# Turning the Delta layer's inputs to tokens block by block, two blocks behind their convolution

## The reference

```
u, qkv, g_in, beta_in, z = split(a @ w_in)
y_ssm = s5_glu(u, ...)                      # hg * sigmoid(hg @ w_glu + b_glu)
qkv = silu(causal_conv(qkv, conv_w))        # 4 taps along the tokens
q, k, v = split(qkv, 3)
q = l2norm(q per head) * 128 ** -0.5
k = l2norm(k per head)
beta = sigmoid(beta_in)
g = -exp(a_log) * softplus(g_in + dt_bias)  # summed along each chunk
o = gated_delta_chunked(q, k, v, g, beta)
```

## Time and profile before

| what | value |
|---|---|
| median of 3 runs | 3237.29 us (3222.32 to 3237.57) |
| the profiled execution's own time | 3239.65 us |
| its span, first to last instruction | 3238.1 us |
| mean granted TensorE clock | 0.945 |
| TensorE busy (matmul) | 2942.9 us, 91% |
| VectorE busy | 1127.9 us, 35% |
| ScalarE busy | 631.1 us, 19% |

### The profile page before, as it was taken

One profiled execution on the slowest core, in us unless ns is written; L12 is line 12 of the kernel. 1 busy time (PEld: TensorE's weight loads), 2 busy tenths in 40 slices (PEclk: granted clock), 3 DMA queues, 4 the chain that ended last, 5 costly groups with the idle time before them and its releaser, 6 DMA issues. The chain is left out here.

```text
span 3238.1 us, 32792 instructions
## 1 busy us (share of the span) xinstructions
PE 2942.9 (91%) x12473; PEld 1583.8 (49%) x12474; DVE 1127.9 (35%) x2447; ACT 631.1 (19%) x1248; POOL 246.2 (8%) x352
## 2 busy tenths in 40 slices
PE   7999899999799999979799899577897999999798
PEld 5544555545444444434376644367654444444243
DVE  2584355544200000024371623566464000000052
ACT  3310355521100101112211111222211101101030
POOL 0000000001100000020000000134201000000110
PEclk9999899999799999989897799888997999999899
DMA  4000881031699999962110210000414999999641
GB/s 153 26 27 0 328 347 53 1 121 57 241 414 415 421 405 399 397 243 84 52 50 1 37 44 26 1 2 2 165 53 169 415 413 412 410 404 397 235 162 45
DMA packets 138550, 617.24 MB, mean 191 GB/s; under 512 B 25188, under 2 KB 31748, under 8 KB 121992
## 3 DMA queue, kind: packets, MB, share of 16 engines
q1 hardware_dynamic: 110952, 525.93, 41.2%
q0 software_dynamic: 24064, 86.00, 7.0%
q10 hardware_dynamic: 3376, 3.19, 0.3%
HBM read 508.00 MB, written 105.91 MB: 190 GB/s over the span
## 5 line engine op out<-in xcount | busy, mean ns | idle before, releaser
L1974 PE MATMUL acc<-wg,xt 128*128 128x512 f32 x512 | 222.9, 598 | 0.0
L737 PE MATMUL acc<-h,xt 128*128 128x512 f32 x384 | 165.2, 592 | 0.0
L2572 PE MATMUL acc<-xt,slabs 128*128 128x512 f32 x384 | 165.1, 592 | 0.0
L1974 PEld LDWEIGHTS acc<-wg,xt 128*128 128x128 f32 x512 | 98.5, 193 | 123.2 <-issue 123.2
L376 PE MATMUL scores<-qkt 65*128 65x512 f32 (+7 forms) x384 | 148.9, 498 | 0.9 <-DVE qkt L516 0.9
L522 DVE TENSOR_REDUCE nmax<-scores 128x1 f32<-128x256 f32 (+7 forms) x128 | 96.8, 756 | 77.5 <-PE scores L378 76.2
L1720 PE MATMUL py<-place 128*64 128x512 f32 (+1 forms) x352 | 120.2, 594 | 1.0 <-DVE place L1800 1.0
L1720 PE MATMUL pu<-place 128*128 128x512 f32 (+1 forms) x320 | 119.8, 593 | 0.0
L2572 PEld LDWEIGHTS acc<-xt,slabs 128*128 128x128 f32 x384 | 72.9, 190 | 91.4 <-issue 91.4
L737 PEld LDWEIGHTS acc<-h,xt 128*128 128x128 f32 x384 | 72.9, 190 | 91.1 <-issue 90.9
L1243 PE MATMUL acc<-place 128*128 128x512 f32 x256 | 114.3, 601 | 2.7 <-PEq L75 2.7
(11 more groups left out here) (645 smaller groups left out, 5170.1 us busy)
## 6 DMA issues: line engine op xcount, KB each, us to landing
own<-in_moe_w_gate_dram SPq DMA_DIRECT2D x22, 2048.0 KB, 16.3
place<-in_moe_w_down_dram SPq DMA_DIRECT2D x22, 2048.0 KB, 16.3
place<-in_moe_w_up_dram SPq DMA_DIRECT2D x20, 2048.0 KB, 18.2
slots_out<-zeros SPq DMA_DIRECT2D x4, 9216.0 KB, 62.8
place<-in_moe_w_gate_dram SPq DMA_DIRECT2D x18, 2048.0 KB, 21.2
own<-in_moe_w_up_dram SPq DMA_DIRECT2D x16, 2048.0 KB, 16.0
own<-in_moe_w_down_dram SPq DMA_DIRECT2D x10, 2048.0 KB, 19.5
xt<-in_moe_w_gate_dram SPq DMA_DIRECT2D x9, 2048.0 KB, 22.4
```

Source lines behind the costliest of these rows:

```text
L737: last = pe.matmul(acc[:, n % 4, 0:width], xs[:, k, tile_of(i)], weights[:, k, cols], start=(k == 0), stop=(k == k_of - 1))
L1974: last = pe.matmul(acc[:, u % 4, :], xt[:, k, i * P:(i + 1) * P], wg[:, k, n * SLAB:(n + 1) * SLAB], start=(k == 0), stop=(k == KD - 1))
L2572: last = pe.matmul(acc[:, n % 4, :], slabs[:, s % 2, k, (m % 4) * P:(m % 4 + 1) * P], xt[:, k, half * SLAB:(half + 1) * SLAB], start=(k == ...
```

## The change

`gdn_to_tokens` is gone, and with it the second of the stages above. `delta_inputs` takes the place of `project_convolved` and does both jobs by blocks of 128 channels. Between the two products of block m TensorE turns block m - 2 (8 transposes into two PSUM banks, `tokens`); ScalarE copies it to its place in token order with one operation over 1024 columns; VectorE squares and sums it behind the convolution of block m; ScalarE takes its 8 roots one block later, and VectorE scales it. The factor of q is folded into the sum before the root. `gdn_masks`, `load_rows` and `gdn_gates` stand in the same joint stage as `s5_glu` and `delta_inputs`: 29 semaphores and one meeting. The gates' matmul (`sums`) stands on TensorE behind block 0, their copy (`sums_out`) on VectorE ahead of the first convolution. Places move too: q, k and v lie in `h` and `gdn_t`, and a new `work` of 12 blocks holds the weight slabs, the gate's input and later what `h`, `gdn_t` and `qkv` held.

```diff
--- before.py
+++ after.py
-def s5_glu(nc, c, t, j, y, out_t, joint):
+def s5_glu(nc, c, t, j, y, hgt, sig, out_t, joint):
-        hgt = sbuf(nc, ctx, "hgt", [P, KC, S])
-        sig = sbuf(nc, ctx, "sig", [P, 2, SLAB])
...
-def project_convolved(nc, c, xt, w, conv_w, out_t, joint):
+def delta_inputs(nc, c, xt, w, conv_w, slabs, squares, qkv, sums, sums_out, joint):
...
+        out = sbuf(nc, ctx, "out", [P, 3, S])
+        taps_raw = out[0:GDN_CONV].rearrange("p a n -> p (a n)")[:, 0:3 * GDN_W]
+        ms, length = [sbuf(nc, ctx, n, [P, NORMED, NT]) for n in ("ms", "length")]
         acc = psum(nc, ctx, "acc", [P, 4, SLAB])
...
+        tokens = psum(nc, ctx, "tokens", [P, 2 * SLAB])
+        with stage(nc, "slab0_in", "slab1_in", "taps_in", "taps_turned", "taps_out", "products", "copied", "convolved",
+                   "activated", "turned", "to_tokens", "squared", "roots", "vec_steps", joint=joint) as (
+                       block, (slab0_in, slab1_in, taps_in, taps_turned, taps_out, products, copied, convolved, activated, turned,
+                               to_tokens, squared, roots, vs)):
...
+            def place(m):
+                return qkv[m // GDN_HEADS][:, :, m % GDN_HEADS, :]
             @block.sync
             def _(sp):
...
+                sp.dma_start(taps_raw, conv_w).then_inc(taps_in, 16)
...
+                    sp.dma_start(slabs[s % 2], w_v[:, :, s * SLAB:(s + 1) * SLAB]).then_inc(slab_in[s % 2], 16)
             @block.tensor
             def _(pe):
+                def product(m, half):
...
+                def turn(m):
+                    pe.wait_ge(activated, m + 1)
+                    if m:
+                        pe.wait_ge(to_tokens, m)
+                    else:
+                        pe.wait_ge(taps_out, 2)
+                    for i in range(NT):
+                        last = pe.transpose(tokens[:, i * P:(i + 1) * P], out[:, m % 3, i * P:(i + 1) * P], c.ident[:])
+                    last.then_inc(turned, 1)
                 pe.wait_ge(taps_in, 16)
                 for m in range(blocks):
...
+                    last = pe.transpose(tokens[:, m * GDN_CONV:(m + 1) * GDN_CONV], taps_raw[:, m * P:(m + 1) * P], c.ident[0:GDN_CONV, 0:GDN_CONV])
                 last.then_inc(taps_turned, 1)
                 for m in range(blocks):
...
+                        pe.wait_ge(slab_in[m // 4 % 2], 16 * (m // 8 + 1))
+                    product(m, 0)
+                    if m >= 2:
+                        turn(m - 2)
+                    product(m, 1)
+                    if m == 0:
+                        sums(pe, tokens[:, SLAB:SLAB + NT * GDN_HEADS])
+                turn(blocks - 2)
+                turn(blocks - 1)
             @block.scalar
             def _(act):
+                def evacuate(m, half):
+                    act.wait_ge(products, 2 * m + half + 1)
+                    if m >= 2:
+                        act.wait_ge(convolved, m - 1)
+                    act.activation(raw[:, m % 2, PAD + half * SLAB:PAD + (half + 1) * SLAB], acc[:, (2 * m + half) % 4, :], ACT.Copy).then_inc(copied, 1)
                 def silu(m):
                     act.wait_ge(convolved, m + 1)
...
+                    act.activation(out[:, m % 3, :], out[:, m % 3, :], ACT.Silu).then_inc(activated, 1)
+                def copy(m):
+                    act.wait_ge(turned, m + 1)
+                    act.activation(place(m), tokens[:].rearrange("p (t d) -> p t d", t=NT), ACT.Copy).then_inc(to_tokens, 1)
+                def root(m):
+                    act.wait_ge(squared, m + 1)
+                    act.activation(length[:, m, :], ms[:, m, :], ACT.Sqrt).then_inc(roots, 1)
                 for m in range(blocks):
...
+                    evacuate(m, 0)
+                    if m >= 2:
+                        copy(m - 2)
+                    if 3 <= m < NORMED + 3:
+                        root(m - 3)
+                    evacuate(m, 1)
                     if m:
                         silu(m - 1)
                 silu(blocks - 1)
+                copy(blocks - 2)
+                copy(blocks - 1)
             @block.vector
             def _(dve):
                 step = Steps(dve, vs)
...
+                def convolve(m):
                     dve.wait_ge(copied, 2 * m + 2)
-                    o = out_t[m]
+                    if m >= 3:
+                        dve.wait_ge(turned, m - 2)
+                    o = out[:, m % 3, :]
...
+                def lengths(m):
+                    dve.wait_ge(to_tokens, m + 1)
+                    step(dve.tensor_tensor(squares, place(m), place(m), ALU.mult))
+                    step(dve.tensor_reduce(ms[:, m, :], squares, AX.X, ALU.add))
+                    dve.tensor_scalar(ms[:, m, :], ms[:, m, :], EPS, float(GDN_HD) if m < GDN_HEADS else 1.0, ALU.add, ALU.mult).then_inc(squared, 1)
+                def scale(m):
+                    dve.wait_ge(roots, m + 1)
+                    step(dve.reciprocal(length[:, m, :], length[:, m, :]))
+                    step(dve.tensor_tensor(place(m), place(m), length[:, m, :].unsqueeze(2).to_broadcast([P, NT, GDN_HD]), ALU.mult))
+                dve.wait_ge(taps_turned, 1)
+                dve.tensor_copy(taps[:].rearrange("p m a -> p (m a)"), tokens[:, 0:blocks * GDN_CONV]).then_inc(taps_out, 1)
+                dve.wait_ge(taps_out, 1)
+                sums_out(dve, tokens[:, SLAB:SLAB + NT * GDN_HEADS]).then_inc(taps_out, 1)
+                dve.memset(raw[:, 0, 0:PAD], 0.0)
+                step(dve.memset(raw[:, 1, 0:PAD], 0.0))
+                for m in range(blocks):
+                    convolve(m)
+                    if 2 <= m < NORMED + 2:
+                        lengths(m - 2)
+                    if 3 <= m < NORMED + 3:
+                        scale(m - 3)
...
+def gdn_gates(nc, c, t, j, gb, g, joint):
...
+        with stage(nc, "in", "negated", "exped", "logged", "summed", "vec_steps", joint=joint) as (
...
-                dve.wait_ge(summed, 1)
-                step(dve.tensor_copy(g.sums[:], ps[:]))
...
+            def sums(pe, out):
                 pe.wait_ge(logged, 1)
+                pe.matmul(out, c.upto[:], s[:].rearrange("p t h -> p (t h)"), start=True, stop=True).then_inc(summed, 1)
+            def sums_out(dve, out):
+                dve.wait_ge(summed, 1)
+                return dve.tensor_copy(g.sums[:].rearrange("p t h -> p (t h)"), out)
+    return sums, sums_out
...
-def gdn_to_tokens(nc, c, qkvt, qkv, joint):
...
-        qkvt = [h[:, m] for m in range(NT)] + [gdn_t[:, m] for m in range(4)]
-        with joint_stage(nc) as joint:
-            s5_glu(nc, c, t, j, output_of(u), s5_t, joint)
-            project_convolved(nc, c, xt, w_in[:, OD_QKV:OD_G], t["gdn_conv_w"][j], qkvt, joint)
         def tiles(block4):
             return block4.rearrange("p k n -> p (k n)").rearrange("p (t h d) -> p t h d", t=NT, h=GDN_HEADS)
-        wt, qt, scratch = tiles(h[:, 0:4]), tiles(h[:, 4:8]), tiles(gdn_t[:])
+        qkv = (tiles(h[:, 0:4]), tiles(h[:, 4:8]), tiles(gdn_t[:]))
...
+            work = sbuf(nc, heads, "work", [P, 12, S])
+            wt, qt, scratch = [tiles(work[:, n:n + 4]) for n in (0, 4, 8)]
...
             with ExitStack() as prepare:
+                k = Masks()
+                gdn_mask_places(nc, k, prepare)
                 with joint_stage(nc) as joint:
-                    k = gdn_masks(nc, c, prepare, joint)
+                    gdn_masks(nc, c, k, joint)
+                    sig = sbuf(nc, joint.memory, "sig", [P, 2, SLAB])
+                    s5_glu(nc, c, t, j, output_of(u), work[:, 8:12], sig, s5_t, joint)
                     load_rows(nc, [(gains[:], t["gdn_o_norm"][j])], joint)
-                    gdn_to_tokens(nc, c, qkvt, qkv, joint)
-                gdn_gates(nc, c, t, j, gbz, g)
+                    sums, sums_out = gdn_gates(nc, c, t, j, gbz, g, joint)
+                    delta_inputs(nc, c, xt, w_in[:, OD_QKV:OD_G], t["gdn_conv_w"][j], [slab_place(work[:, 0:4]), slab_place(work[:, 4:8])],
+                                 sig[:].rearrange("p a n -> p (a n)").rearrange("p (t d) -> p t d", t=NT), qkv, sums, sums_out, joint)
                 gdn_prepare(nc, c, g, k, qkv, wt, qt, intra_t, scratch)
-            slab0 = slab_place(gdn_t[:])
+            slab0 = slab_place(work[:, 8:12])
             gdn_scan(nc, c, g, qkv, wt, qt, intra_t, o, gbz[:, :, OD_Z - OD_G:], gains[:], [(slab0, slab_of(t["od_w_out"][j], 0))])
-            flat, room = qkv[:].rearrange("p t a h d -> p (t a h d)"), xt[:, 0:4].rearrange("p k n -> p (k n)")
-            m, rest = flat[:, 0:NT * D].rearrange("p (t d) -> p t d", t=NT), flat[:, NT * D:]
-            slab1 = rest.rearrange("p (k n) -> p k n", k=KD)
+            room, m, slab1 = xt[:, 0:4].rearrange("p k n -> p (k n)"), work[:, 0:NT], slab_place(gdn_t[:])
...
-            places = [s5_t[:], gbz[:], xt[:, 0:4], xt[:, 4:8], gdn_t[:]]
```

(30 more changed lines are left out.)

84 lines of the change are left out of this document (13 added, 71 removed).

## The result

| | before | after |
|---|---|---|
| median of 4 runs | 3237.23 us (3222.32 to 3237.57) | 3195.84 us (3185.32 to 3205.38) |
| the profiled execution's own time | 3239.65 us | 3205.38 us |
| its span | 3238.1 us | 3203.8 us |
| mean granted TensorE clock | 0.945 | 0.949 |

The ratio is 0.9889, with a 95% interval from 0.9857 to 0.9922: 1.1% less, and clear of 1. The forecast was 3205, the range 3190 to 3221. The four runs of after lie in two pairs (3185.32 and 3187.40; 3204.28 and 3205.38), and before has single runs 15 us under the others too, so the median of after lies in a gap; where the two clusters come from is told with the last experiments. The profiled executions of both kernels are of the upper cluster, and they differ by 34.3 us.

A forecast was written before the change was run, and what follows sets the result against it. TensorE bounds the Delta inputs' products; behind them other engines set the end in turn. Pieces of 8.9 + 0.3 + 1.0 + 1.9 + 1.0 + 0.3 + 2.2 = 15.6 us replace 49.1, giving 3206.2 profiled; forecast 3205, range 3190 to 3221.

The forecast's parts named there:

- The place and the sum: From the last Silu to the preparation's first transposes, 49.1 us would be replaced by pieces of 15.6 us: 33.5 less.
- The turns: Ten groups of 8 transposes among the Delta inputs' products cost TensorE 8.9 us; two more stand behind the last product.
- the experts' rows: MoE profile rows where 8 transposes stand among 128x512 products, taken as the cost of one turn: 0.89 us.
- the interpolation by the number of semaphores: Meeting at the joint stage's end, clearing 29 semaphores: put at 2.2 us, between 1.4 for 16 and 2.8 for 40.
- The gates' matmul: Two 128x32 records on TensorE behind block 0: put at 0.3 us, between 0.2 and 0.64.
- Their chain: VectorE's small gate operations end at about 1900.5 us, 3.9 us before TensorE asks behind block 0, so cost nothing.
- The hidden work: Added work per block, ScalarE's 4.9 to 5.2 us and VectorE's 4.1, lies under products; uncovered it costs 32 us.
- The spare of 3.9 us per Silu: Silu is ready 3.0 us into a block and its turn comes at 6.9, so turns are not late.
- Turns that hold TensorE up (1): At the turns among the products, late Silus make TensorE wait, losing half the gain: 3223 us, chance 0.06.
- The clock (2): Behind each turn the next half block runs at 1.2 instead of 2.4 GHz: 69 us more, 3275, chance 0.04.
- The give-back (3): The MoE's transfers set its pace from a fixed point, so the earlier start is waited off: 3239 us, chance 0.04.
- Dearer small pieces (4): Small pieces at the joint, or a late gates' chain at block 0, cost 5 to 10 us more: 3212 to 3216.

The follow-up runs named there:

- the last experiments: Wide 128x512 products added ahead of the S5 chunks' small matmuls; with four, the kernel before took 3224.14 us, after 3191.61, after with a shorter stage end 3185.98.
- the doubled kernel: The changed kernel with each of the ten turns among the products done twice (16 transposes into the same place): 3213.36 us, ratio 0.9935.
- +3.3 us: The changed kernel with five unused 512-column copies on ScalarE ahead of each Silu of blocks 0 to 9: 3185.77 us in one run, stage 186.88 us.
- +6.6: The changed kernel with ten unused 512-column copies on ScalarE ahead of each Silu of blocks 0 to 9: 3237.71 us in one run, stage 217.82 us.

## Why the prediction was right

- **The place and the sum.** 49.1 us were to be replaced by 15.6, and 15.3 came: 33.8 us less where 33.5 was forecast. Two of the pieces that it hides or removes were put back one by one and cost 10.2 and 27.6 us, where 10.2 and 28 were expected. The profiled execution was to take 3206.2 and took 3205.38. That the medians of before and after were 41 us apart (3237.23, 3195.84) and not 34 is the clusters' doing: two of four runs of after lay in the lower one.
- **The turns.** 0.89 us each from the experts' rows; 0.87 here, in after and again for the added ones in the doubled kernel. The two waits behind the last product cost as foreseen: block 11's turn 1.94 at the lower clock, its copy 1.02, and 2.2 us from the copy's end at 2074.99 to 2077.18, as the interpolation by the number of semaphores gave. Copy, turn, copy and meeting took 6.24 us from the end of Silu (2070.94); 6.4 with the handoffs was the forecast.
- **The gates' matmul.** Put at 0.3, the row says 0.30, but only 0.14 of it (1904.19 to 1904.33) lies between products, since it overlaps with the next one: sized twice too large, and a little under its lower bound of 0.2. Their chain was done 4.9 us before it was needed; 3.9 was forecast.
- **The hidden work.** The spare of 3.9 us per Silu holds (3.7 in the trace): nothing at +3.3 us, and 2.67 us of waiting at +6.6. Shown by two kernels, not only argued. What it hides was put at 32 us (8 x 4) if its cover were gone; 27.6 is what it costs at the stage's end, with ScalarE's roots still under VectorE's squares.
- **The rivals.** Turns that hold TensorE up (1): absent here and at 3.3 us of delay, real at 6.6. The clock (2): it stays at 1.00 at twice the transposes; the only falls that were seen at turns (1.7 us, twice in ten) came behind waits of 2.7 us, of which after has none. The give-back (3): the stages behind take 1126.6 us, before 1127.1. Dearer small pieces (4): none was off by more than 0.2.
- **What the prediction had no term for, and where luck came in.** It treated the low run of before as scatter and only widened the range by it (3190 to 3221). Two of the four runs of after lie below that range, at 3185.32 and 3187.40, and the median of 3195.84, at which no run lies, is the middle of a gap. With three of four in the lower cluster it would have been near 3187 and out of the range. So the stage and the profiled time were forecast by their mechanism; that the median fell inside the range was partly luck. 33.5 off both clusters of before, 3220 to 3223 and 3236 to 3243, would have given 3187 to 3190 and 3203 to 3210 for single runs, and even that leaves out 3185.32.

## What to carry to other kernels

When a serial stage behind a TensorE-bound one is moved among its products, add up each helper engine's duties per block, and find the one moment at which TensorE asks for their result; if each engine's duties fit into a block (8.8 us of VectorE's in 14.6 here) and the spare at that moment is positive (3.9 us here), the moved work costs only TensorE's own part. Look at what the moved transposes release and not at them: without cover for squares and scaling 27.6 of the 33.8 us are gone. And before a median is trusted, line up all runs: where they fall in two heaps, find the stretch that differs, or compare stages within profiles.

## What the runs showed of the hardware

Behind a stop of 1.97 us TensorE's granted clock can stay near the 1.2 GHz level for some 40 us of work that keeps it busy all the time, where that work is small matmuls (64x16 by 64x128, with four transposes ahead of each group): 0.54 over 45 us with 44.85 busy. Or it can be 1.00 from the start; which of the two comes changes from one execution to the next, and it is worth 16 to 20 us in the kernels with several runs of each kind. With four products of 128x512 ahead, the clock was back at 1.00 before the small matmuls started even where it had fallen, and it was 0.99 or 1.00 from 1742 to 1768 us in every profile of them. All 18 runs with four ahead (and 4 with one ahead of each group) lay in one cluster. Why the clock falls behind the stop in some executions only stays open; no run here tells.

Float32 transposes of 128x128 among dense 128x512 products cost 0.87 us per 8 and left the granted clock at 1.00, even at 16 in a row; by themselves they brought it from 0.50 to 0.99 in the stage of turns before.
